# Block attention: a step's transposed weights copied out of PSUM by DVE and ACT, one bank each, where DVE copied both

## What is computed

```python
s_c = einsum("bgrtd,bgnd->bgrtn", qn, k_cmp) * scale        # compressed branch
p_c = masked_softmax(s_c, ...);  o_c = p_c @ v_cmp
s_s = einsum("bgrtd,bgtkld->bgrtkl", qr, k_g) * scale       # selected blocks
p_s = masked_softmax(s_s, mask_s);  o_s = p_s @ v_g
s_w = einsum("bgrtd,bgsd->bgrts", qr, kwb) * scale          # window
p_w = masked_softmax(s_w, mask_w);  o_w = p_w @ vwb
return gt[..., 0:1] * o_c + gt[..., 1:2] * o_s + gt[..., 2:3] * o_w
```

## Time and profile before

| what | value |
|---|---|
| median of 3 runs | 1049.11 us (1046.52 to 1052.4) |
| the profiled execution | 1047.47 us, span 1045.5 us from first to last instruction |
| granted TensorE clock, mean | 0.995 |
| busy share PE, DVE, ACT, POOL | 97%, 72%, 50%, 14% |
| attention steps | from about 776 to 833 us of the span |

### The profile page before, as it was taken

How to read it: one execution, slowest core, us unless ns; L and a number is a source line. 1 busy time by engine, 2 the same in 40 slices (tenths; PEclk the granted TensorE clock), 3 DMA queues, 4 the chain that set the end, 5 groups by cost and what they waited for, 6 DMA issues and landing times. The chain is left out here.

```text
span 1045.5 us, 22435 instructions
## 1 busy us (share of the span) xinstructions
PE 1018.1 (97%) x8533; PEld 966.4 (92%) x8533; DVE 749.9 (72%) x1198; ACT 524.6 (50%) x900; POOL 146.0 (14%) x194
## 2 busy tenths in 40 slices
PE   8999989999999999989999999999999999999998
PEld 8999779999999999858999999998976799999998
DVE  5877867666666666885777777778877587777775
ACT  6453755644444454226644444456646464444442
POOL 0070010012222100002001000140115401000000
PEclk9999999999999999999999999999999999999999
DMA  9563225265655646632555555664620055555551
GB/s 350 161 202 100 74 75 177 87 210 188 198 200 188 196 140 186 189 123 81 183 200 187 196 182 205 201 174 144 223 101 22 1 171 183 191 184 190 189 189 51
DMA packets 51041, 169.71 MB, mean 162 GB/s; under 512 B 5664, under 2 KB 10784, under 8 KB 50848
## 3 DMA queue, kind: packets, MB, share of 16 engines
q1 hardware_dynamic: 45216, 163.22, 47.7%
q10 hardware_dynamic: 5760, 5.57, 2.0%
HBM read 162.15 MB, written 1.05 MB: 156 GB/s over the span
## 5 line engine op out<-in xcount | busy, mean ns | idle before, releaser
L1561 DVE TENSOR_TENSOR WL<-WR,WH 128x1024 fp32r<-128x1024 f32 x302 | 373.7, 1255 | 141.0 <-ACT WH L1294 138.6
L861 PE MATMUL acc<-XH,WH 128*128 128x256 f32 x1360 | 386.8, 284 | 3.1 <-DVE XP L1578 1.9
L862 PE MATMUL acc<-XL,WH 128*128 128x256 f32 x1360 | 378.1, 278 | 0.0
L863 PE MATMUL acc<-XH,WL 128*128 128x256 f32 x1360 | 378.0, 278 | 0.0
L1294 ACT ACTIVATE WH<-WR 128x1024 fp32r<-128x1024 f32 x302 | 312.7, 1051 | 91.1 <-PE acc L863 58.2
L861 PEld LDWEIGHTS acc<-XH,WH 128*128 128x128 f32 x1360 | 255.4, 188 | 7.1 <-DVE WL L1561 3.6
L863 PEld LDWEIGHTS acc<-XH,WL 128*128 128x128 f32 x1360 | 256.9, 189 | 0.0
L862 PEld LDWEIGHTS acc<-XL,WH 128*128 128x128 f32 x1360 | 255.9, 188 | 0.9
L861 PE MATMUL big<-UH,WH 128*128 128x256 f32 x608 | 168.7, 278 | 0.0
L862 PE MATMUL big<-UL,WH 128*128 128x256 f32 x608 | 168.7, 277 | 0.0
L863 PE MATMUL big<-UH,WL 128*128 128x256 f32 x608 | 168.7, 277 | 0.0
(11 more groups left out here) (301 smaller groups left out, 1360.1 us busy)
## 6 DMA issues: line engine op xcount, KB each, us to landing
WR<-weights SPq DMA_DIRECT2D x302, 512.0 KB, 3.6
STK<-UP ACTq DMA_DIRECT2D x32, 138.0 KB, 3.6
X<-x_t SPq DMA_DIRECT2D x4, 256.0 KB, 6.2
MEM<-mem_t SPq DMA_DIRECT2D x1, 1024.0 KB, 9.6
result_t<-X SPq DMA_DIRECT2D x4, 256.0 KB, 2.1
CON<-constants SPq DMA_DIRECT2D x1, 880.0 KB, 11.7
CBUF<-KCV ACTq DMA_DIRECT2D x4, 128.0 KB, 5.4
CBUF<-KCV ACTq DMA_DIRECT2D x4, 127.5 KB, 7.0
```

The costliest lines, as they stand in the source:

```text
L861: pe.matmul(out, wh, hi, start=start, stop=False, skip_group_check=True)
L862: pe.matmul(out, wh, lo, start=False, stop=False, skip_group_check=True)
L863: return pe.matmul(out, wl, hi, start=False, stop=stop, skip_group_check=True)
L1561: dve.tensor_tensor(WL[:, cs % SPL], WR[:, cs % RAW], WH[:, cs % SPL].bitcast(F32), ALU.subtract).then_inc(w_low, 1)
```

## The change

The copy of a step's transposed weights is split by bank. ACT copies bank 0 (head 0, 384 columns) with an `activation` of kind Copy, behind the exponentials of its iteration and ahead of its `YH`. DVE copies bank 1 (head 1, 384 columns) where it copied both. The semaphore `at_pt` becomes two, `at_pt_act` and `at_pt_dve`; PE waits for both, ahead of a turn and ahead of the outputs. ACT's copy has the same two waits as DVE's: that the turn is done, and that the outputs which read the same half of `PT` two steps ago are done. The work on PE and POOL is the same.

```diff
             def turn(i):
                 pe.wait_ge(sem("at_pn"), i + 1)
                 if i >= 1:
-                    pe.wait_ge(sem("at_pt"), i)
+                    pe.wait_ge(sem("at_pt_act"), i)
+                    pe.wait_ge(sem("at_pt_dve"), i)
...
-                pe.wait_ge(sem("at_pt"), i + 1)
+                pe.wait_ge(sem("at_pt_act"), i + 1)
+                pe.wait_ge(sem("at_pt_dve"), i + 1)
                 for m in range(2):
                     for e in range(2):
...
                     act.activation(PCT.rearrange("p s t -> p (s t)"), acc[:, 1, :], ACT.Copy).then_inc(sem("pct_done"), 1)
+                if 3 <= i <= STEPS + 2:
+                    act.wait_ge(sem("at_t"), i - 2)
+                    if i >= 5:
+                        act.wait_ge(sem("at_o"), i - 4)
+                    act.activation(PT[:, (i - 3) % 2, 0], mis[:, 0, 0:384], ACT.Copy).then_inc(sem("at_pt_act"), 1)
                 if i >= 6 and i % 2 == 0:
...
                     if i >= 5:
                         dve.wait_ge(sem("at_o"), i - 4)
-                    dve.tensor_copy(PT[:, (i - 3) % 2], mis[:, :, 0:384]).then_inc(sem("at_pt"), 1)
+                    dve.tensor_copy(PT[:, (i - 3) % 2, 1], mis[:, 1, 0:384]).then_inc(sem("at_pt_dve"), 1)
```

## The result

The changed kernel takes 1059.73 us (median of 17 runs, 1052.16 to 1067.54), the kernel before 1050.32 us (17 runs beside them): ratio 1.0095, 95% interval 1.0077 to 1.0112. So it is slower by 9.4 us, in the direction of the forecast and at almost twice its size; 1059.73 lies just above the range. The profiled execution took 1057.07 us, span 1055.1.

What follows compares the result with a forecast made beforehand. PE was taken to bound the steady attention steps. Five pairs at 6.87 us plus start and end steps put iteration 16's turn 5.09 us later; with 0.05 more the sum was 5.1 us, 1054.2 us, range 1050.0 to 1058.5.

Steps and rivals of the forecast that it cites:

- What bounds the kernel: Steady attention steps: PE alone sets the pace, 6.12 us for two iterations; DVE's copy is ready 0.55 us early.
- DVE's lighter copy: DVE's copy halved to 384 columns: about 0.55 us against 0.95, 0.4 us less per iteration, worth nothing in the steady part.
- The price of ACT's copy: ACT's added copy of 384 columns from PSUM: 0.51 us, between 0.39 and 0.63.
- The place of the copy: ACT's copy stands behind four exponentials, so the next turn cannot start before 3.27 us after DVE's reductions start.
- the circle of one copy: Odd reductions to even turn 3.27 us, turn to next odd reductions 3.60: 6.87 us a pair instead of 6.12.
- A second path: From even reductions through ACT's copy, YH and YL to the odd reductions: 4.02 us, just inside about 4.1, deciding nothing.
- R(9): Start of DVE's reductions of iteration 9.
- R(8): Start of DVE's reductions of iteration 8.
- T(4): Start of the turn in PE's iteration 4, where PE waits 0.99 us for DVE's copy before the change.
- The start: First turn that waits for the copy, iteration 4: ACT's copy would make it 0.31 us late.
- The clock: Rival: clock falls in the stall ahead of iteration 16's turn, plus 1.3 us, 6.4 in all, 1055.5 us; chance 0.30.
- Not slower: Rival: both engines copy at once, saving 0.8 us at iteration 4 and in the last iterations, 1048.3 us; chance 0.06.

Runs made afterwards that it cites:

- act_128: Changed kernel with ACT copying only the first 128 of its 384 columns, the other 256 copied by nobody; executed once, 1053.39 us, 6.64 us a pair.
- yh_first: Changed kernel with YH ahead of ACT's copy in even iterations; executed once, 1054.18 us, 6.86 us a pair.
- four_pp: Changed kernel with four weight buffers in place of three; executed once, 1053.90 us, 6.86 us a pair.
- best2: ACT's copy ahead of the exponentials, plus DVE's first copy earlier and five filler passes ahead of iteration 2's scores; ratio 0.9995 to the kernel before.
- after_again: The changed kernel run again without edit, for a second profile; ratio 1.0079 to the kernel before, 7.01 us a pair.
- after_look4: A further profile of the changed kernel without edit; its six profiles have 62.13 to 67.92 us for the attention steps.
- after_look5: Another further profile of the changed kernel without edit; its six profiles have 62.13 to 67.92 us for the attention steps.
- dve_both: Changed kernel with both banks copied by DVE, as two instructions with two semaphores; ratio 1.0004 to the kernel before, 6.12 us a pair.
- fill_tail: Changed kernel with filler matmuls only ahead of the turn of iteration 16, plus one more wait ahead of even turns; ratio 1.0085, 7.15 us a pair.

## Why the prediction was right or wrong

**What bounds the kernel: right.** DVE's lighter copy (0.553 us against about 0.55 forecast) was worth nothing in the steady part; DVE waits longer for YH instead (1.91 us against 1.19).

**The price of ACT's copy: right,** 0.50 against 0.51. By act_128 it also was the smaller part of the matter.

**The place of the copy and the circle of one copy: right, but not the longest.** Its length was forecast at 6.87 and measured at 6.86 in three places: in the first pair of the changed kernel (792.29 to 799.15), where no YH stands between, in yh_first and in four_pp.

**"A second path ... reaches R(9) at R(8) + 4.02 ... runs just inside it and decides nothing": this is the step of the schedule that failed.** It started the even exponentials at R(8) + 1.06, as soon as the maxima were there. But they have a second wait, for the turn whose buffer they overwrite. It is in the code beside L606, and in the trace of before it never comes last in the steady part: there the turn is early. Once the even turn is late, it does: 807.10 - 805.49 = 1.61 us behind the reductions of iteration 8 in place of 1.06. With 1.61 the path would have been 1.61 + 1.60 + 0.37 + 0.44 + 0.42 = 4.44 behind R(8), outside the circle's own (4.1 in the prediction, and 806.16 + 3.60 - 805.49 = 4.27 by the rows of this profile), and the pair 7.00. From T(4) to T(16) that makes 41.90 us where 41.22 was forecast and 36.44 stood before. The start took 0.18 of the 0.31 us given to it (first scores to T(4) 13.13, before 12.95). Together the turn of iteration 16 comes 5.64 us later than before, against 5.09. The sign that the prediction had given for this case failed too: it expected every turn to wait if YH and YL carried the delay, and they carried it with only the even turns waiting.

**The clock: put at nothing in the sum, the larger of the two steps that failed.** As a rival it was the right one, given too little: it had a chance of 0.30 and a price of 1.3 us; the traces have it in five of six executions, at 1.0 to 2.6 us above before, with a mean of 1.36 over the six. The stall itself came as priced there, 1.99 us, where 1.98 had been worked out and 1.9 taken. What spoke for the fall (after PE's waits of 1.6 and 2.5 us the clock was down) should have weighed more than the remark that 1.9 is nearer to the short waits. And the short wait without a fall was read from one execution: the wait of 1.42 us near 467 has a fall beside it in the three other profiles of the same kernel. That a fall there could last twice as long as the one I priced, as in two of the five, I had not considered.

**The sum in these terms.** Schedule 5.55; falls behind the turn of iteration 16, mean over the six profiles 1.45 above 7.10; the long fall in one of them, mean 0.5: 7.5 us. The mean times of all timed executions, 38 of the changed kernel and 93 of the one before, differ by 1058.9 - 1050.5 = 8.4 us, with a standard error of 0.6, and the mean clocks are 0.988 and 0.991 (for before over the 76 that have it on record). So the profiles place all but about 1 us, which the scatter of runs and profiles covers. Of the 9.4 us of the first set, which is the slowest set of the changed kernel, 2 are placed by no profile. The forecast of 5.1 was the schedule part, nearly; the range had been drawn for the clock at one price, and the time fell 1.2 us outside it.

**Not slower: wrong for this kernel,** since ACT's copy ended 0.7 us after the turn would have been ready. That the copy has to be waited for, for two engines to help each other, is what the kernel with the copy ahead of the exponentials shows from the other side: both halves in time and no gain. Of the Trainium skill's two rules neither gives this result. The one that gives elementwise work without a transcendental to VectorE (ScalarE: Activation LUTs, Rules for kernel authors) has the sign right here for a reason that the rows don't bear out, 0.50 us on ACT against 0.55 on DVE for the same 384 columns; by the one on using both engines (TensorEngine Tiling (Array Packing), PSUM Bottleneck) both placements of the copy would be an improvement, and the ratios are 1.0095 behind the exponentials and 0.9994 ahead of them.

## What to carry to other kernels

Work given to a less busy engine costs by its place in that engine's order first, and by its length only where the place is on the path: 0.50 us behind the exponentials cost 0.88 us a pair, and the same instruction ahead of them nothing. When a step becomes late, list again every wait on it, also those that never come last in the trace of before; here it was the reuse of a buffer, and it closed a longer circle than the one that started the delay. And where a change opens a stall of about 2 us on PE, price the clock behind it at once and not as a remote case.

## What the runs showed of the hardware

After PE's wait of 1.98 or 1.99 us the granted clock was at 0.5 (1.2 GHz) in five of six executions of the same kernel, from 0.3 to 1.3 us after PE had resumed, in three of them for 3.4 us and in two for 6.8. With filler matmuls that left 0.45 us of the wait, neither of two profiles shows a fall there; nor does one after a wait of 1.63, 1.79 or 1.84 us at the same place (act_128, yh_first and four_pp, one profile each). Since one of the six had no fall either, two profiles make it likely, and no more, that the fillers prevented it.

The length of a wait alone does not decide. The clock also fell near shorter ones: in all 17 profiles with PE's wait of 1.58 us ahead of the scores of iteration 2 it fell, at the end of that wait or up to 6.4 us behind it (in best2, where fillers left 0.47 us of the wait, it did not), and at a wait of 1.42 us near 467 it fell in three of four executions of the kernel before. Nor did a longer one always bring a fall: PE waits 2.64 us near 138 in every profile of both kernels, and in after_again, after_look4 and after_look5 none follows there. What in PE's work around a wait makes the difference is open.

A fall costs less than half its length where PE waits for a chain anyway: 1.1 us for one of 3.4 us and 2.7 for one of 6.8, both behind the turn of iteration 16. The one near 785 costs nothing in the kernel before: it lasts 3.4 us in three profiles and 6.8 in the fourth, and the steps take 56.57 to 56.60 us in all four. One wait more in PE's order, which cost nothing where PE ran through (6.12 us a pair in dve_both), went with 0.15 us more a pair where PE stood still (fill_tail); why is open.
